# A hybrid attention and MoE block: sigmoid on ScalarE, state updates under a suffix product, and a shorter low-rank gate

## The reference

```python
h = rmsnorm(x, g_mix)
qg, kg, vg, glr, rg, qs, ks_, vs = split(h @ w_in)      # 256, 256, 512, 16, 512, 512, 512, 512 columns
log_a = log_sigmoid(glr @ w_gla_gate + b_gla_gate) / 16
o_gla = gla_group(qg / 8, kg, vg, log_a)                # 4 heads, chunks of 64 tokens:
#   U = (k * exp(G_end - G))^T v ; state = exp(G_end) * state + U ; o = q @ state
o_gla = rmsnorm(o_gla, g_gla_head) * silu(rg)
# stick breaking, 8 heads of 64: z = q k^T / 8, strictly causal
#   A[t, s] = exp(log_sigmoid(z[t, s]) + sum over s < j < t of log_sigmoid(-z[t, j])) ; o_sb = A v
x = x + concat([o_gla, o_sb]) @ w_out
x = x + cross_attention(rmsnorm(x), rmsnorm(mem))
x = x + moe(rmsnorm(x))                                 # top 4 of 32 experts
return rmsnorm(x, g_final)
```

## Time and profile before

| | |
|---|---|
| median of three runs | 1660.09 us |
| the profiled execution | 1662.74 us |
| its span, first to last instruction | 1661.0 us |
| TensorE busy | 1618.1 us, 97% |
| VectorE busy | 1095.2 us, 66% |
| ScalarE busy | 834.9 us, 50% |
| GpSimd busy | 117.1 us, 7% |
| mean granted TensorE clock | 0.984 of full |

### The profile page before, as it was taken

One profiled execution on the slowest core, in us unless ns is written; L12 is line 12 of the kernel. 1 busy time (PEld: TensorE's weight loads), 2 busy tenths in 40 slices (PEclk: granted clock), 3 DMA queues, 4 the chain that ended last, 5 costly groups with the idle time before them and its releaser, 6 DMA issues.

```text
span 1661.0 us, 27037 instructions
## 1 busy us (share of the span) xinstructions
PE 1618.1 (97%) x10113; PEld 1373.8 (83%) x10113; DVE 1095.2 (66%) x1197; ACT 834.9 (50%) x838; POOL 117.1 (7%) x214
## 2 busy tenths in 40 slices
PE   7999789998999999999999999999999999999997
PEld 6878678986888888888888888888888888888885
DVE  4233665435278777776777777777777777777766
ACT  5265447424234554555455554545555555545554
POOL 0011110000000100000010010000001001000000
PEclk9999899999979999999999999999999999999999
DMA  6111143411659999999999999999999999999993
GB/s 211 51 51 51 51 152 127 152 55 62 254 204 302 365 359 379 365 374 380 361 372 364 378 378 359 379 361 369 366 383 373 373 362 372 363 373 374 372 374 118
DMA packets 134630, 476.31 MB, mean 287 GB/s; under 512 B 10289, under 2 KB 10338, under 8 KB 134562
## 3 DMA queue, kind: packets, MB, share of 16 engines
q1 hardware_dynamic: 125874, 449.29, 72.5%
q0 software_dynamic: 7056, 24.78, 6.2%
q10 hardware_dynamic: 1664, 1.74, 0.3%
HBM read 457.30 MB, written 18.48 MB: 286 GB/s over the span
## 4 chain that ended last, share of the span: by engine, by line
PE 96%; DVE 3%; ACT 1%; issue 0%; DMA 0%; DVEq 0%; ACTq 0%
PE psum L1088 24%; PE psum L1115 22%; PE psum L1147 21%; PE psum L673 17%; PE psum L730 1%; PE psum L844 1%; PE psum L1074 1%; PE psum L1082 1%; PE psum L882 1%; PE psum L966 1%; PE psum L986 1%; DVE ring L1741 1%; PE psum L692 0%; PE psum L832 0%; PE psum L1005 0%; PE psum L1198 0%
## 5 line engine op out<-in xcount | busy, mean ns | idle before, releaser
L1088 PEld LDWEIGHTS psum<-MIX,ring 128*128 128x128 f32 x4096 | 775.4, 191 | 101.6 <-DVE MIX L2198 2.0
L1088 PE MATMUL psum<-MIX,ring 128*128 128x96 f32 x4096 | 726.1, 259 | 1.7 <-DVE MIX L2198 1.7
L2157 DVE TENSOR_TENSOR ring_split<-ring,w_hi_a 128x2048 fp32r<-128x2048 f32 x64 | 146.4, 2288 | 84.3 <-ACT w_hi_a L1527 84.3
L1115 PE MATMUL psum<-ring_split,xs_hi 128*96 128x512 f32 x512 | 199.4, 435 | 0.0
L2169 DVE TENSOR_TENSOR ring_split<-ring,w_hi_x 128x2048 fp32r<-128x2048 f32 x62 | 141.8, 2288 | 84.8 <-ACT w_hi_x L1538 84.8
L1147 PE MATMUL psum<-ring_split,act_hi 128*96 128x512 f32 x508 | 196.8, 435 | 0.0
L2157 DVE TENSOR_TENSOR ring_split<-ring,w_hi_x 128x2048 fp32r<-128x2048 f32 x64 | 146.4, 2289 | 72.0 <-ACT w_hi_x L1527 72.0
L2169 DVE TENSOR_TENSOR ring_split<-ring,w_hi_a 128x2048 fp32r<-128x2048 f32 x62 | 141.6, 2284 | 0.0
L673 PE MATMUL psum<-ring_split,H_hi 128*128 128x512 f32 (+1 forms) x448 | 136.0, 389 | 5.2 <-DVE VGb L1762 3.1
L1527 ACT ACTIVATE w_hi_a<-ring 128x2048 fp32r<-128x2048 f32 x62 | 117.7, 1898 | 21.1 <-DMA ring<-in_w_gu 21.1
L1555 ACT ACTIVATE xs_hi<-MIX 128x768 fp32r<-128x768 f32 x32 | 27.0, 845 | 191.4 <-DVE MIX L2184 189.5
(11 more groups left out here) (333 smaller groups left out, 2718.4 us busy)
## 6 DMA issues: line engine op xcount, KB each, us to landing
ring<-in_w_gu SPq DMA_DIRECT2D x256, 1024.0 KB, 10.5
ring<-in_w_down SPq DMA_DIRECT2D x128, 1024.0 KB, 12.2
ring<-in_w_in SPq DMA_DIRECT2D x5, 2048.0 KB, 9.2
X<-in_x SPq DMA_DIRECT2D x8, 512.0 KB, 8.2
ring<-in_w_out SPq DMA_DIRECT2D x2, 2048.0 KB, 8.4
ring<-in_w_mk SPq DMA_DIRECT2D x2, 2048.0 KB, 8.7
ring<-in_w_mv SPq DMA_DIRECT2D x2, 2048.0 KB, 7.6
ring<-in_w_mq SPq DMA_DIRECT2D x2, 2048.0 KB, 8.3
```

Of the source, the lines that this page charges most:

```text
L1088: return mm(psum[:, dst, q * C:(q + 1) * C], lhsT=gate_w(k // 2)[:, k % 2, f * P:(f + 1) * P], rhs=xsT[:, k, :], start=k == 0 and q == 0, ...
L1115: x_last = mm(psum[0:C, L0 + half, :], lhsT=rows_, rhs=cols_, start=k == 0 and n == 0, stop=k == KT - 1 and n == 2, skip_group_check=True)
L2157: v.tensor_tensor(lin_lo(c), lin_w(c), chunk_hi(c).bitcast(F32), ALU.subtract)\
```

## The change

Four things, all in the mixing stage.

1. **Low-rank gate in one pass.** High and low part of the 16 weight columns stand side by side in one tile of 32 columns, so two matmuls for each inner tile (activations high and low) replace three. The product has 32 rows, high and low, and the gate matmul sums them by having the gate weights twice, over 33 rows instead of 17. One more small load fills the second copy. The term low times low, left out before, is in.
2. **Sigmoid by exp and ln on ScalarE.** exp(-ln(1 + exp(-x))), three ScalarE instructions instead of one; VectorE keeps only the multiplication.
3. **State updates under a suffix product.** U 2 and 3 go from behind both suffix products of pair 2 to between them, and VectorE runs the update of states 0 to 3 ahead of head 5's low part.
4. **Order in pairs 2 and 3.** VectorE copies rg 1 between the two halves of the low part of out0 and gates after av_out(2); the O 0 1 copy stands before the softplus of head 6. `sb_out(3)` goes from before the out projection to between its f = 4 and f = 5, and TensorE's wait for the last `sb_exp` ahead of f = 4 stays. ScalarE's list has the sigmoids, `og_rstd(0)`, the exponentials of heads 6 and 7 and mix_hi in a new order. VectorE gates tile 2 and makes the low part of f = 4 before it copies O 1 0 and O 1 1, and runs gla_gate(1) before the low part of f = 7.

```diff
@@ FILL
-    [("vg", 3), ("rg", 0), ("U", 0), ("U", 1)], [("U", 2), ("U", 3), ("rg", 1)],
+    [("vg", 3), ("rg", 0), ("U", 0), ("U", 1)], [("rg", 1)],
+BETWEEN = [("U", 2), ("U", 3)]
@@ SP: loads
-                    sp.dma_start(w_gate[16:17, :], b_gla_gate[0:1, :]).then_inc(s_small, 16)
+                    sp.dma_start(w_gate[16:32, :], w_gla_gate[0, :, :]).then_inc(s_small, 16)
+                    sp.dma_start(w_gate[32:33, :], b_gla_gate[0:1, :]).then_inc(s_small, 16)
@@ TensorE: fill
-                    done(contract_split(b[0:16, :], lambda lo, k: (w_glr_lo if lo else w_glr_hi)[:, k, :],
-                                        all_rows))
+                    for k in range(KT):
+                        for lo in range(2):
+                            last = mm(b[0:32, :], lhsT=w_glr_r[:, k, :], rhs=all_rows(lo, k),
+                                      start=k == 0 and lo == 0, stop=k == KT - 1 and lo == 1)
+                    done(last)
-                        last = mm(b[:, u * 256:(u + 1) * 256], lhsT=glrT[0:17, i * P:(i + 1) * P],
-                                  rhs=w_gate[0:17, :], start=True, stop=True)
+                        last = mm(b[:, u * 256:(u + 1) * 256], lhsT=glrT[0:33, i * P:(i + 1) * P],
+                                  rhs=w_gate[0:33, :], start=True, stop=True)
@@ TensorE: head pairs
                 sb_suffix(2 * p)
+                if p == 2:
+                    for g in BETWEEN:
+                        fill(g)
                 sb_suffix(2 * p + 1)
                 for g in FILL[2 * p + 1]:
                     fill(g)
-                sb_out(p)
-                pe.wait_ge(s_sba, 2 * p + 2)
                 if p + 1 < PAIRS:
+                    sb_out(p)
+                    pe.wait_ge(s_sba, 2 * p + 2)
                     sb_scores(p + 1)
+            pe.wait_ge(s_sba, SB_HEADS)
@@ TensorE: out projection
             for f in (4, 5, 6, 7):
+                if f == 5:
+                    sb_out(PAIRS - 1)
@@ ScalarE
-                go(silu_t[i % 2], rg[:, i, :], ACT.Exp, scale=-1.0).then_inc(s_rgexp, 1)
+                t = silu_t[i % 2]
+                ch.link(go(t, rg[:, i, :], ACT.Exp, scale=-1.0))
+                ch.link(go(t, t, ACT.Ln, bias=one_col[:, :]))
+                go(t, t, ACT.Exp, scale=-1.0).then_inc(s_rgexp, 1)
-            pair_weights(2)
-            rg_exp(0)
+            pair_split(2)
+            rg_sigmoid(0)
+            sb_exp(4)
+            sb_exp(5)
             split_chunk_hi("out0")
-            rg_exp(1)
-            pair_weights(3)
+            rg_sigmoid(1)
+            pair_split(3)
+            act.wait_ge(s_ghead, 16)
+            og_rstd(0)
+            rg_sigmoid(2)
+            sb_exp(6)
             mix_hi(4)
             mix_hi(5)
+            sb_exp(7)
             mix_hi(6)
-            rg_exp(2)
-            rg_exp(3)
+            rg_sigmoid(3)
             og_rstd(1)
             mix_hi(7)
@@ VectorE
-                ch.link(v.tensor_scalar_add(t, t, 1.0))
-                ch.link(v.reciprocal(t, t))
-                v.tensor_tensor(rg[:, i, :], rg[:, i, :], t, ALU.mult).then_inc(s_rgd, 1)
+                v.tensor_tensor(rg[:, i, :], rg[:, i, :], silu_t[i % 2], ALU.mult).then_inc(s_rgd, 1)
             fill(("rg", 0))
+            fill(("U", 1))
             sb_split_lo(5)
-            fill(("U", 1))
             fill(("U", 3))
+            split_lo("out0", 0)
             fill(("rg", 1))
+            split_lo("out0", 1)
+            av_out(2)
             rg_gate(0)
-            split_chunk_lo("out0")
-            av_out(2)
             rg_gate(1)
             fill(("O", 0, 0))
+            fill(("O", 0, 1))
             sb_softplus(6)
-            fill(("O", 0, 1))
             sb_softplus(7)
             sb_split_lo(6)
             fill(("rg", 2))
             sb_split_lo(7)
             fill(("rg", 3))
             gla_gate(0)
+            rg_gate(2)
+            mix_lo(4)
             fill(("O", 1, 0))
             fill(("O", 1, 1))
-            mix_lo(4)
             mix_lo(5)
             mix_lo(6)
-            rg_gate(2)
+            rg_gate(3)
             av_out(3)
-            rg_gate(3)
+            gla_gate(1)
             mix_lo(7)
-            gla_gate(1)
```

More of the change, by code:

```diff
@@ L117, in plan_banks @@
         for part in (0, 1):
-            for g in FILL[2 * p + part]:
+            for g in (BETWEEN if 2 * p + part == 5 else []) + FILL[2 * p + part]:
                 plan.add(g, "act" if g in ACT_FILL else "dve", pool=(6, 7))
@@ L198, in build @@
         KDb = sb("KDb", [P, 1024])
-        glr_at = nc.sbuf_base
-        w_glr = sb("w_glr", [P, KT, 16])
-        w_glr_hi = sb("w_glr_hi", [P, KT, 16], F32R)
+        w_glr_r = sb("w_glr_split", [P, KT, 32], F32R)
         ident = sb("ident", [P, P])
@@ L213, in build @@
         gcols = sb("gcols", [P, 4 * KT + 1])
-        w_gate = sb("w_gate", [17, 256])
+        w_gate = sb("w_gate", [33, 256])
         ssq = sb("ssq", [P, 32])
@@ L221, in build @@
         gain_rows = RGb[0:4 * KT, 0:P]
+        w_glr = MIX[:, 5, 0:KT * 16].rearrange("p (k c) -> p k c", k=KT)
         bgu_rows = MIX[0:E, 0:4, :].rearrange("p a b -> p (a b)")
@@ L230, in build @@
         silu_t = [scratch[:, a:a + 512] for a in (7232, 5120)]
-        glrT = KDb[0:32, 0:512]
+        glrT = KDb[0:33, 0:512]
         kd = KDb[:, :].rearrange("p (i c) -> p i c", i=TT)
@@ L332, in build @@
         H_lo = nc.alloc_sbuf_tensor_at("H_lo", [P, KT, T], F32R, offset=x_at)
-        w_glr_lo = nc.alloc_sbuf_tensor_at("w_glr_lo", [P, KT, 16], F32R, offset=glr_at)
         MIX_lo = nc.alloc_sbuf_tensor_at("MIX_lo", [P, KT, T], F32R, offset=mix_at)
@@ L1275, in _ @@
             split_chunk_hi("k")
-            act.wait_ge(s_small, 48)
-            go(w_glr_hi[:, :, :], w_glr[:, :, :], ACT.Copy).then_inc(s_ahi, 1)
+            act.wait_ge(s_small, 64)
+            go(w_glr_r[:, :, 0:16], w_glr[:, :, :], ACT.Copy).then_inc(s_ahi, 1)
             for j in (1, 3):
@@ L1310, in fill, with rg_sigmoid @@
                     took(g, go(decay[:, :], b[:, 0:16], ACT.Exp))
-            def rg_exp(i):
+            def rg_sigmoid(i):
                 wait_emptied(act, ("rg", i))
@@ L1364, in mix_hi, with pair_split @@
                 go(H_hi[:, f, :], MIX[:, f, :], ACT.Copy).then_inc(s_ahi, 1)
-            def pair_weights(p):
+            def pair_split(p):
                 sb_log(2 * p)
@@ L1370, in pair_weights @@
                 sb_split_hi(2 * p + 1)
[L1371 to L1377, removed]
+            pair_split(0)
+            sb_exp(0)
+            sb_exp(1)
             gate_log()
@@ L1380, in _ @@
             split_chunk_hi("vg")
-            pair_weights(1)
+            pair_split(1)
+            sb_exp(2)
+            sb_exp(3)
             for g in FILL[3]:
@@ L1689, in _ @@
             dve.wait_ge(s_ahi, hi_count(("glr",)))
-            v.tensor_tensor(w_glr_lo[:, :, :], w_glr[:, :, :], w_glr_hi[:, :, :].bitcast(F32),
+            v.tensor_tensor(w_glr_r[:, :, 16:32], w_glr[:, :, :], w_glr_r[:, :, 0:16].bitcast(F32),
                             ALU.subtract).then_inc(s_alo, 1)
@@ L1737, in rg_gate @@
             def rg_gate(i):
-                t = silu_t[i % 2]
                 dve.wait_ge(s_rgexp, i + 1)
-                ch.link(v.tensor_scalar_add(t, t, 1.0))
-                ch.link(v.reciprocal(t, t))
-                v.tensor_tensor(rg[:, i, :], rg[:, i, :], t, ALU.mult).then_inc(s_rgd, 1)
+                v.tensor_tensor(rg[:, i, :], rg[:, i, :], silu_t[i % 2], ALU.mult).then_inc(s_rgd, 1)
             def fill(g):
@@ L1751, in fill @@
                 elif kind == "glrT":
-                    took(g, v.tensor_copy(glrT[0:16, :], b[0:16, :]))
+                    took(g, v.tensor_copy(glrT[0:32, :], b[0:32, :]))
                 elif kind == "qg":
```

## The result

The kernel after takes 1640.88 us (median of 4, 1637.4 to 1644.48) where the kernel before takes 1660.25 (4 runs): a ratio of 0.9885, 95% interval 0.9873 to 0.9897. The forecast was 1640.4, with a range of 1637.0 to 1645.8. The profiled execution of after took 1644.48 us, span 1642.7, and is the longest of the four, so its sums run 3.6 us above the median.

The account below looks back on a forecast made before the run. TensorE was taken as the bound, losing time to VectorE waits and low clock in the mixing stage. Savings of 17.9 and 1.8 us made 19.7, taken off the 1660.09 us median: 1640.4, range 1637.0 to 1645.8.

Parts of the forecast that it names:

- Bound: Mixing stage: TensorE bounds; five waits on VectorE, 14.1 us in all, with reciprocals on the chain, plus lost clock.
- Part 1: Low-rank gate: eight fewer matmuls at 0.232 us, 1.8 us saved, bounds 0 and 1.9.
- Part 2: U 2 and 3 between pair 2's suffix products: 2.1 us stall gone, clock stays up, rg 1 ends 185.5, not 190.6.
- Part 3: Sigmoid on ScalarE: 2.05 us each, no table load; rg 2 waits 0.1 us instead of 3.1.
- rival C: The logarithm brings two 1.28 us table loads in each sigmoid, costing 3.3 us: 1643.7; chance 0.07.
- Rival B: Early state update does not fit; suffix 5 waits behind U 3 and the clock falls: 1644.9; chance 0.10.
- Part 4: Before the out projection: new 2.7 us TensorE wait on ScalarE's exponentials, clock falls, 2.3 us lost; projection ends at 241.6.
- the forecast case: The clock falls in the new stall before the out projection, costing 2.3 us more: 1640.4; chance 0.62.
- rival A: The clock does not fall in the new stall before the out projection, returning 2.3 us: 1638.1; chance 0.17.
- The sum: Whole kernel: 17.9 us in the mixing stage from the later parts plus 1.8 from the gate, 19.7 us saved.
- the cross-check: Mixing stage: stalls and lost clock, 22.4 us, less the new stall with its clock, 5.0, and 0.1: 17.3 us.

Follow-up runs that it names:

- the two later groups: The kernel after, unchanged, run again beside the kernel before: 1643.11 us (ratio 0.9896) and 1643.88 us (ratio 0.9895).

## Why the prediction was right

**Bound.** Right: the waits named in the earlier trace rows were the ones to go, and that the reciprocals caused most of three of them is shown by the sigmoid alone (0.9912) and the sigmoid undone (a wait of 6.9 us). The order of part 4 was tested only in the place of sb_out(3) and of the last exponentials; what its other moves give was not taken apart.

**Part 1.** 1.8 us forecast; 16 matmuls in 3.81 us where 24 took 5.57, and pair 1's last suffix product 1.7 to 1.8 us earlier. Right in the place, and 1.2 us in the median.

**Part 2.** rg 1 was worked out to start at 180.0 and started at 180.12. The stall with its clock, 5.1 us, came back as 4.7 when the part was undone. The stall is right; the 3.0 us of clock is the dearest of the five profiles that have it (0.2 to 3.0), so there the forecast took one execution for the rule.

**Part 3.** 2.05 us a sigmoid forecast, 0.62 + 0.72 + 0.63 and two gaps measured, 2.04; the logarithm, taken at 0.72 between 0.63 and 1.37, took 0.72. The wait ahead of rg 2 was forecast at 0.1 and is 0.3. The only table load of the mixing stage is the one at 0.80, as before: rival C did not occur. Rival B, with a margin of 0.4 us, did not either: suffix 5 starts right behind U 3.

**Part 4.** The one new wait stands where it was put, 2.3 us for a forecast 2.7. The step that is not right as it stood is its clock: I took the fall as given, from two stretches that fell and one that did not. The copies mix_hi(4) and (5) took 1.03 us together; two at the 0.63 of the row that the forecast names would be 1.3, so its 1.1 was right without following from its row. In three profiles of after the fall came once. Over all profiles, waits of 2.1 us brought it down in four of five, and one of 1.2 us did once, where 1.0 in before did not: the length of the wait alone does not decide it. So the forecast case and rival A are one kernel in different executions, and the width of the range (8.8 us) was needed for what is spread of the clock: the four runs of after lie within 7.1 us. In the profiled execution rival A's 2.3 us came in, part 1's 1.6 and 2.3 later went out.

**The sum.** 19.7 us forecast; 19.4 measured by the medians, 17.4 and 16.7 by the two later groups. That it held so closely in the first is in part luck of the clock: the three groups together give 17.8, and the cross-check of 17.3, made from stalls and lost clock alone, is nearer to that. One reason for the excess may lie in the method (it was not tested): the gain was sized on a profiled run 2.65 us above the median, with its dear clock behind the stalls, and then taken off the median.

## What to carry to other kernels

Where TensorE waits for a copy that frees a PSUM bank, look at what stands ahead of that copy in its engine's list: here 3.36 us reciprocals, four in all, held up copies of 0.7 us, and 2.0 us each on a half-idle engine replaced them. Two cures of one wait do not add up (here the 4.6 and the 3.3), so undo each alone before counting both. After such a change, ask which queue now ends last: putting two exponentials ahead of a sigmoid that nobody was waiting for gave more than a low-rank product with a third fewer matmuls.

## What was not expected of the hardware

The clock falls without a wait. In seven of thirteen profiles it went to 1.2 GHz for part of the time right behind 2 us of two-column matmuls during which TensorE counts as busy, and cost 1.6 us, and in the others not, with the same instructions. Short stalls behave alike. Of four profiles with a stall of 2.2 to 2.3 us ahead of the out projection, two lost nothing more, one 1.5 us and one 2.8. Of five with a stall of 2.1 us ahead of rg 1, one lost 0.2 and two 3.0. One profile is therefore not enough to say what a stall of 2 us costs. GpSimd's four masks took 1.03 us beside an idle VectorE and 1.9 to 2.3 beside its subtractions with two SBUF inputs.
